# Order of work in a delta rule chunk's first slots, the first output projection's units begun on the attention's features, and a bias table's transfers in eight parts

## The chip, the cores and the metric

One NeuronCore of a Trainium2 chip runs the whole program. The metric is the device time of one execution in microseconds, lower is better. TensorE is written PE here, its weight loads PEld, VectorE is DVE, ScalarE is ACT, GpSimd is POOL and SyncE is SP.

## The reference, cut to what matters

Three transformer blocks are run one after the other on 1024 tokens of 1024 features, all in float32. The first block matters here:

```
x = layer_norm(x);  h = x @ w_in
o_gdn = gated_delta_rule(q, k, v, g, beta), forward and backward in time, 4 heads of 128, then rms_norm * silu(z)
o_na  = neighborhood_attention(q, k, v, rpb), 16 rows of 64 tokens, 8 heads of 64, then rms_norm
x = layer_norm(alpha * x + concat(o_gdn, o_na) @ w_out);  x = layer_norm(alpha * x + relu(x @ w1 + b1)^2 @ w2 + b2)
```

In a chunk of the delta rule a unit lower triangular system is solved, then `o = q_dec S + qk v_new` and `S = S * g_last + k_dec^T v_new`. The second block has a sliding window attention whose score bias is a table looked up by distance (`rel_bias[bucket]`). It is laid out once, long before it is used.

## The kernel before

Every large matrix product is cut into *units*: 128x1024 weights, fetched by SP into one of four slots (`load_sp`, L252), split into a high part on ACT (`split_act`, L257) and a low part on DVE (`split_dve`, L262), and multiplied in three passes (high by high, high by low, low by high): 24 matmuls of 512 columns (L299) for an output unit. A slot's next load is issued when PE has done the unit in it, so loads run four units ahead. Splits run two units ahead (`AHEAD`). `walk` writes each engine's instruction stream from one list of steps. Every engine works its own stream strictly in order, and the streams meet at semaphores.

**The mixers.** Between the first input projection and the first output projection PE works two mixers interleaved in slots. The delta rule (`gdn_pe`, `gdn_act`, `gdn_dve`) has 8 steps `n` of 14 slots `s`; each step handles one 128-token chunk for both directions: `d = 0` takes chunk `n`, `d = 1` takes chunk `7 - n`. The attention (`na_pe`, `na_act`, `na_dve`) takes one of the 16 rows every 7 slots. Each direction has three PSUM banks, `gbank(d, 0)` to `gbank(d, 2)`. In a chunk's slots:

- slot 12 and 13: prepare the next chunk's decay and `A`, solve for `v_new` (`V`, copied to `g_vn` by ACT, L1121);
- slot 0: PE forms the output of the *previous* chunk (`o`, L1020 and L1021, 16 matmuls a direction, bank 1) and its state update (`su`, 4 matmuls, bank 0), then turns the new `A` (bank 2, L1007). DVE copies or adds the output (L1138, L1141), updates the state `g_S` (L1146), and then forms the first level of the inverse from the turned `A` (`lev`, L1152, and `Dt`, L1158);
- odd slots 1 to 11, levels `l` = 1 to 6: PE turns `Dt` (bank 0, L1007) and multiplies by `A` (`Q`, bank 1, L1001), ACT copies the turned part (`g_D`, L1097), DVE masks `Q` (L1164). Even slots 2 to 12: PE forms `X` (bank 2, L1001), DVE subtracts it from `Dt` (L1171).

On PE the turn of level 1 waits for `Dt`, so behind it stands all of PE's later work. From the second half of the chunks on, a third thread (`gout`) normalises finished chunks beside this (sums L1428 on PE, L1432 and L1434 on ACT). Slot 0 of `n` = 6 and 7 has such a piece.

**The end of the mixers.** In the last slot (`n = 8`, slot 0) the last outputs and the last attention row are formed. Then `end1_pe`, `end1_act` and `end1_dve` normalise the last three chunks (`out_sq`, `out_sum`, `out_rs`, `out_norm`; chunk 0, then 6, then 7) and split the mixed features of the first 512 tokens, then of the last 512, into high and low parts (`mix1_hi` on ACT, L1475; `mix1_lo` on DVE, L1481). Features 4 to 7 of 8 are the attention's and come first in `MIX_ORDER`; 0 to 3 are the delta rule's. Only behind all this do ACT and DVE split the first weights of `out1[0]`, the output projection's eight units of the first half, which PE then works. SP issues, ahead of those weights and on the same queue, the 4 MB of residual (`xT<-x`, L1584).

**The bias table.** `t5_pool` runs on POOL. It broadcasts an 8-partition table into an internal DRAM tensor by one DMA (1.5 MB, L1635), waits, and reads it back skewed by one DMA (1 MB, L1638). DVE waits for it 38 units after PE made the table (L1657).

Of the kernel before, what the change touches and what calls it, by code (L numbers as in the profile page):

```python
# [14 lines left out]
P = 128  # L15
# [105 lines left out]
def build_program(nc, g):  # L121

    ctx = ExitStack()
    with ctx:
# [78 lines left out]
        class Unit:  # L203

            def __init__(self, kind, src=None, half=0, j=0, gr=0, pool="bg", meta=False, gate=None):
                self.kind, self.src, self.half, self.j, self.gr, self.pool = kind, src, half, j, gr, pool
                self.meta, self.gate, self.n = meta, gate, None
                self.ks, self.back, self.whole = range(DC), None, kind in WHOLE
# [60 lines left out]
        def unit_pe(pe, u):  # L269
            if u.kind == "nv1":  # L270
                nv1_pe(pe, u)
                return
            if u.use:
                pe.wait_ge(bank_free(u), u.use)
# [4 lines left out]
            if u.kind == "down":  # L279
# [10 lines left out]
                return  # L290
            for h in range(2) if u.whole else [u.half]:
                spans = [(0, W // 2), (W // 2, W)] if u.meta else [(META, W)]
                for i_k, k in enumerate(u.ks):
# [7 lines left out]
            last.then_inc(mm_done[u.z], 1)  # L301
# [646 lines left out]

        def level(n, d, l):

            return 2 * NL * n + 2 * l + d + 1
# [41 lines left out]
        def gdn_pe(pe):  # L993
# [15 lines left out]

            pe.wait_ge(nv_act, 4)  # L1010
            pe.wait_ge(nv_dve, 4)
            for n, s in gdn_slots():
                m, l = n - 1, (s + 1) // 2
                if s == 0 and n:
                    for d in (0, 1) if n < TC else (1, 0):
                        pe.wait_ge(gs["vn"], once(m, d))
                        pe.wait_ge(gs["qd"], once(m, d))
                        for h in range(GH):
                            o = pbank(gbank(d, 1))[:, h, :]
                            nc.tensor.matmul(o, g_S[d][:, h, :], g_qd[d][:, h, :], start=True, stop=False)  # L1020
                            last = nc.tensor.matmul(o, g_vn[d][:, h, :], g_qk[d][:, m % 2, h, :], start=False, stop=True)  # L1021
                        last.then_inc(gs["o"], 1)
                        if n < TC:
                            pe.wait_ge(gs["eg"], once(n, d))
                            pe.wait_ge(gs["t0"], once(n, d))
                            pe.wait_ge(gs["kd"], once(m, d))
                            heads(gbank(d, 0), g_kd[d], g_vn[d]).then_inc(gs["su"], 1)
                if s == 0 and n < TC:
                    for d in range(2):
                        pe.wait_ge(gs["A"], once(n, d))  # L1030
                        turned(gbank(d, 2), g_A[d]).then_inc(gs["AT"], 1)
                if 1 <= s <= 12 and s % 2 and n >= 0:
                    for d in range(2):
                        pe.wait_ge(gs["Dt"], level(n, d, l - 1))
                        if l == 1:
                            pe.wait_ge(gs["S"], once(n, d))
# [4 lines left out]
                        turned(gbank(d, 0), g_Dt[d]).then_inc(gs["tr"], 1)  # L1041
# [2008 lines left out]
```

## Time and profile before

| | |
|---|---|
| three timed runs | 4097.46, 4099.32, 4105.66 us (median 4099.32) |
| the profiled execution | 4106.44 us, of which 4104.7 us span |
| PE busy | 3958.7 us, 96% of the span |
| DVE, ACT busy | 2167.2 us, 1676.0 us |
| mean granted clock of PE | 0.985 |
| delta rule's and attention's slots | about 421 to 966 us of the span |
| end of the mixers to the output projection's first matmul | about 966 to 992 us |

A busy share says how long an engine had an instruction in work, not that it went at full speed: PEclk, the granted clock, has two levels, and at 0.50 a matmul takes twice as long though PE counts as fully busy. In a timeline a line gives the start, the time taken, engine, source line, operation and count; in brackets stand the engine's idle time before it and what ended that.

### The profile page before, as it was taken

What the parts mean: (1) busy time and instruction counts of PE and PEld (TensorE: products, weight loads), DVE (VectorE), ACT (ScalarE), POOL (GpSimd) and SP (SyncE); (2) the same over time, 40 slices, a digit from 0 to 9 for tenths busy, and PEclk for the clock granted to TensorE, in tenths of its full rate; (3) what the DMA queues carried; (4) which work ended last, traced back from release to release, by engine and by line L of the source; (5) the groups of instructions that cost most, each with busy time, mean ns of one, the idle gap of its engine ahead of it and who ended that gap; (6) DMA issues with size and microseconds to landing.
All of it is one profiled execution on the core that took longest, in us unless ns stands there. A gap on an engine that the chain in (4) does not pass through costs nothing.

```text
span 4104.7 us, 47331 instructions
## 1 busy us (share of the span) xinstructions
PE 3958.7 (96%) x19500; PEld 3228.7 (79%) x19500; DVE 2167.2 (53%) x3208; ACT 1676.0 (41%) x2626; POOL 9.9 (0%) x20
## 2 busy tenths in 40 slices
PE   4999999997989999999999999999999999999999
PEld 2777888986778877887787878987778777778887
DVE  6541444554643355784657855436656445645334
ACT  3351555565433354433534444333334233334333
POOL 0000000000000000000000000000000000000000
PEclk9999998998999999999999999999999999999999
DMA  4112000002243222222222222222222222223322
GB/s 165 52 62 63 10 5 5 13 24 100 82 103 97 93 88 93 77 84 86 87 93 78 78 93 92 89 89 81 77 84 96 89 91 78 78 87 114 97 93 87
DMA packets 113565, 323.44 MB, mean 79 GB/s; under 512 B 26656, under 2 KB 33712, under 8 KB 113352
## 3 DMA queue, kind: packets, MB, share of 16 engines
q1 hardware_dynamic: 111416, 314.91, 23.9%
q0 software_dynamic: 1936, 5.51, 0.7%
q8 instruction: 156, 2.56, 0.3%
q14 instruction: 57, 0.47, 0.0%
HBM read 303.86 MB, written 18.06 MB: 78 GB/s over the span
## 4 chain that ended last, share of the span: by engine, by line
PE 90%; DVE 5%; ACT 3%; issue 1%; DMA 1%; SPq 0%; DVEq 0%; ACTq 0%
PE ps L299 48%; PE ps L286 25%; PE ps L1001 4%; PE ps L1269 1%; PE ps L1007 1%; PE ps L712 1%; PE ps L1246 1%; PE ps L2354 1%; PE ps L996 1%; PE ps L1254 1%; PE ps L1794 1%; PE ps L408 1%; DMA w_raw<-in_w_mlp 1%; DVE a L495 0%; DVE xT L348 0%
## 5 line engine op out<-in xcount | busy, mean ns | idle before, releaser
L299 PE MATMUL ps<-a,w_hi 128*128 128x512 f32 (+1 forms) x6128 | 1879.3, 391 | 33.2 <-issue 15.1
L299 PEld LDWEIGHTS ps<-a,w_hi 128*128 128x128 f32 x6128 | 1128.5, 189 | 309.4 <-issue 37.3
L299 PE MATMUL ps<-a,w_lo 128*128 128x512 f32 (+1 forms) x3064 | 1164.7, 387 | 0.0
L262 DVE TENSOR_TENSOR w_lo<-w_raw,w_hi 128x1024 fp32r<-128x1024 f32 x539 | 658.1, 1221 | 461.3 <-ACT w_hi L257 458.5
L257 ACT ACTIVATE w_hi<-w_raw 128x1024 fp32r<-128x1024 f32 x539 | 563.7, 1050 | 593.2 <-DMA w_raw<-in_w_mlp 367.0
L299 PEld LDWEIGHTS ps<-a,w_lo 128*128 128x128 f32 x3064 | 572.2, 189 | 123.0
L286 PE MATMUL ps<-h_hi,w_hi 128*128 128x512 f32 x1536 | 490.5, 401 | 1.9 <-DVE xT L348 1.9
L286 PE MATMUL ps<-h_hi,w_lo 128*128 128x512 f32 x1536 | 481.4, 395 | 0.0
L286 PE MATMUL ps<-h_lo,w_hi 128*128 128x512 f32 x1536 | 481.2, 395 | 0.0
L343 DVE TENSOR_TENSOR h_lo<-u_sq,h_hi 128x512 fp32r<-128x512 f32 x192 | 132.9, 692 | 486.5 <-ACT h_hi L333 486.5
L348 DVE TENSOR_TENSOR xT<-xT,ps 128x1024 f32<-128x1024 f32 x192 | 234.2, 1220 | 287.4 <-PE ps L286 286.5
L286 PEld LDWEIGHTS ps<-h_hi,w_hi 128*128 128x128 f32 x1536 | 285.9, 189 | 73.2 <-issue 5.8
L286 PEld LDWEIGHTS ps<-h_hi,w_lo 128*128 128x128 f32 x1536 | 289.7, 189 | 66.0
L286 PEld LDWEIGHTS ps<-h_lo,w_hi 128*128 128x128 f32 x1536 | 289.8, 189 | 65.6
L328 ACT ACTIVATE u_act<-ps 128x512 f32<-128x512 f32 x128 | 76.4, 597 | 366.2 <-PE ps L299 366.1
L1767 DVE SCALAR_TENSOR_TENSOR mixh<-c_pad,params,mixh 128x512 f32<-128x512 f32 x240 | 163.7, 744 | 0.0
L332 ACT ACTIVATE u_sq<-u_act 128x512 f32<-128x512 f32 x192 | 121.4, 632 | 17.8 <-ACT u_act L328 0.4
L328 ACT ACTIVATE u_act<-ps,params 128x512 f32<-128x512 f32 x64 | 44.0, 688 | 202.9 <-PE ps L299 202.9
L333 ACT ACTIVATE h_hi<-u_act 128x512 fp32r<-128x512 f32 x192 | 118.0, 615 | 0.0
L354 DVE TENSOR_TENSOR xT<-xT,ps 128x512 f32<-128x512 f32 x48 | 33.0, 687 | 147.0 <-PE ps L299 147.0
L1001 PEld LDWEIGHTS ps<-g_gu,g_D 128*128 128x128 f32 x768 | 96.9, 202 | 9.5 <-issue 9.3
L1001 PE MATMUL ps<-g_Dt,g_A 128*128 128x64 f32 x768 | 98.5, 285 | 0.0
(358 smaller groups left out, 3359.8 us busy)
## 6 DMA issues: line engine op xcount, KB each, us to landing
w_raw<-in_w_mlp SPq DMA_DIRECT2D x384, 512.0 KB, 3.4
w_raw<-in_w_in SPq DMA_DIRECT2D x107, 512.0 KB, 3.5
w_raw<-in_w_out SPq DMA_DIRECT2D x48, 512.0 KB, 3.4
xT<-in_x SPq DMA_DIRECT2D x2, 2048.0 KB, 12.3
x<-xT SPq DMA_DIRECT2D x2, 2048.0 KB, 7.6
xT<-x SPq DMA_DIRECT2D x2, 2048.0 KB, 12.9
rpb_rows<-in_rpb SPq DMA_DIRECT2D x1, 3810.0 KB
z<-staged SPq DMA_DIRECT2D x4, 512.0 KB, 3.8
```

Of the source, the lines that this page charges most:

```text
L257: nc.scalar.activation(w_hi[u.z][:, :], w_raw[u.z][:, :], ACT.Copy).then_inc(w_hi_done[u.z], 1)
L262: nc.vector.tensor_tensor(w_lo[u.z][:, :], w_raw[u.z][:, :], w_hi[u.z][:, :].bitcast(F32), ALU.subtract).then_inc(w_split[u.z], 1)
L286: last = nc.tensor.matmul(ps[:, u.bank + c, :], w[:, k * 256 + c * P:k * 256 + (c + 1) * P], act[:, (u.first + k) % RING, :], start=(k == ...
L299: last = nc.tensor.matmul(ps[:, bank, 0:t1 - t0], w[:, k * P:(k + 1) * P], a[:, h, low, k, t0:t1], start=(i_k == 0 and i == 0), stop=(i_k ...
L328: nc.scalar.activation(u_act[:, s, :], ps[:, u.bank, :], ACT.Relu, bias=bias).then_inc(bank_free(u), 1)
L332: nc.scalar.activation(u_sq[:, s, :], u_act[:, s, :], ACT.Square)
L333: nc.scalar.activation(h_hi[:, u.chunk % RING, :], u_act[:, s, :], ACT.Square).then_inc(hid_hi, 1)
L343: nc.vector.tensor_tensor(h_lo[:, r, :], u_sq[:, u.chunk % 2, :], h_hi[:, r, :].bitcast(F32), ALU.subtract)\
L348: nc.vector.tensor_tensor(two, two, ps[:, u.bank:u.bank + 2, :], ALU.add).then_inc(bank_free(u), 1)
L408: nc.tensor.matmul(ps[:, bank, :], const("ones"), m.q[:, 0, :], start=True, stop=True).then_inc(m.s["sum"], 1)
L1001: last = nc.tensor.matmul(halves(pbank(b), l, which)[:, h], lhsT[:, h, :], halves(rhs[:, :, :], l, which)[:, h], start=True, stop=True)
L1767: nc.vector.scalar_tensor_tensor(y, x, w, y, op0=ALU.mult, op1=ALU.add).then_inc(c_tap, 1)
```

## The change

Five edits. (1) Slot 0: PE works output of `d = 0`, the two turns of `A`, output of `d = 1`, then both state updates; DVE forms `lev` and `Dt` before outputs and state. Since the banks then collide, level 1 uses bank 2 for its turn and bank 1 for `X`, and the wait for the state moves from level 1 to level 2. (2) In the last chunk direction 1 comes first in slot 13, so that chunk 0 is ready first. (3) The order of the attention's rows changes so that the first half's are done after 12 rows; in slot 13 of the last chunk ACT and DVE split the attention's features of the first half and the weights of the first two units of `out1[0]`; after the first sum of `end1`, PE works the first half (four of eight feature blocks) of three units, then the two other sums; later those units are completed. The third unit moves to the bank pool "fg". (4) Each unit of `out1` waits for its feature blocks one by one. (5) The bias table is written by eight DMAs, each waiting for the one before, and read by eight.

```diff
+            if u.taken:
+                unit_part(pe, u, u.taken, DC)
                 return
...
+        def unit_part(pe, u, first, stop):
+
+            if first == 0 and u.taken:
+                if u.use:
+                    pe.wait_ge(bank_free(u), u.use)
+                pe.wait_ge(w_split[u.z], u.turn + 1)
             for h in range(2) if u.whole else [u.half]:
                 spans = [(0, W // 2), (W // 2, W)] if u.meta else [(META, W)]
-                for i_k, k in enumerate(u.ks):
+                for i_k in range(first, stop):
+                    k = u.ks[i_k]
...
+        def both_ways(n):
+
+            return (1, 0) if n == TC - 1 else (0, 1)
+
+        def last_once(n, d):
+            return once(n, 1 - d if n == TC - 1 else d)
+
+        def turn_bank(d, l):
+            return gbank(d, 2 if l == 1 else 0)
+
+        def cross_bank(d, l):
+            return gbank(d, 1 if l == 1 else 2)
...
+            def step_out(m, d):
+                pe.wait_ge(gs["vn"], last_once(m, d))
+                pe.wait_ge(gs["qd"], once(m, d))
+                for h in range(GH):
+                    o = pbank(gbank(d, 1))[:, h, :]
+                    nc.tensor.matmul(o, g_S[d][:, h, :], g_qd[d][:, h, :], start=True, stop=False)
+                    last = nc.tensor.matmul(o, g_vn[d][:, h, :], g_qk[d][:, m % 2, h, :], start=False, stop=True)
+                last.then_inc(gs["o"], 1)
+
+            def step_turned(n, d):
+                pe.wait_ge(gs["A"], once(n, d))
+                turned(gbank(d, 2), g_A[d]).then_inc(gs["AT"], 1)
...
-                if s == 0 and n:
-                    for d in (0, 1) if n < TC else (1, 0):
-                        pe.wait_ge(gs["vn"], once(m, d))
-                        pe.wait_ge(gs["qd"], once(m, d))
-                        for h in range(GH):
-                            o = pbank(gbank(d, 1))[:, h, :]
-                            nc.tensor.matmul(o, g_S[d][:, h, :], g_qd[d][:, h, :], start=True, stop=False)
-                            last = nc.tensor.matmul(o, g_vn[d][:, h, :], g_qk[d][:, m % 2, h, :], start=False, stop=True)
-                        last.then_inc(gs["o"], 1)
-                        if n < TC:
-                            pe.wait_ge(gs["eg"], once(n, d))
-                            pe.wait_ge(gs["t0"], once(n, d))
-                            pe.wait_ge(gs["kd"], once(m, d))
-                            heads(gbank(d, 0), g_kd[d], g_vn[d]).then_inc(gs["su"], 1)
-                if s == 0 and n < TC:
+                if s == 0 and n == 0:
                     for d in range(2):
-                        pe.wait_ge(gs["A"], once(n, d))
-                        turned(gbank(d, 2), g_A[d]).then_inc(gs["AT"], 1)
...
+                if s == 0 and 0 < n < TC:
+                    step_out(m, 0)
+                    step_turned(n, 0)
+                    step_turned(n, 1)
+                    step_out(m, 1)
+                    for d in range(2):
+                        pe.wait_ge(gs["eg"], once(n, d))
+                        pe.wait_ge(gs["t0"], once(n, d))
+                        pe.wait_ge(gs["kd"], once(m, d))
+                        heads(gbank(d, 0), g_kd[d], g_vn[d]).then_inc(gs["su"], 1)
+                if s == 0 and n == TC:
+                    step_out(m, 1)
+                    step_out(m, 0)
                 if 1 <= s <= 12 and s % 2 and n >= 0:
                     for d in range(2):
                         pe.wait_ge(gs["Dt"], level(n, d, l - 1))
-                        if l == 1:
+                        if l == 2:
                             pe.wait_ge(gs["S"], once(n, d))
                         if l == 4:
                             pe.wait_ge(gs["R"], once(n, d))
                         if l == 6:
                             pe.wait_ge(gs["kd"], once(n, d))
-                        turned(gbank(d, 0), g_Dt[d]).then_inc(gs["tr"], 1)
+                        turned(turn_bank(d, l), g_Dt[d]).then_inc(gs["tr"], 1)
...
-                        half_heads(gbank(d, 2), g_D[d], g_gu[d], l, 1 - d).then_inc(gs["X"], 1)
+                        half_heads(cross_bank(d, l), g_D[d], g_gu[d], l, 1 - d).then_inc(gs["X"], 1)
...
+                if s == 13 and n == TC - 1:
+                    act.wait_ge(n_copied, 16 * len(HELD))
+                    act.wait_ge(na["of"], NP * 3)
+                    mix1_hi(act, 0, (0, 1, 2, 3))
+                    split_act(act, ahead1[0])
+                    split_act(act, ahead1[1])
...
-                if s == 0 and n:
-                        dve.wait_ge(gs["o"], 2 * TC - d if n == TC else once(m, d))
...
-                            ins.then_inc(gs["S"], 1)
...
+                if s == 0 and n:
+                    for d in both_ways(m):
+                        dve.wait_ge(gs["o"], last_once(m, d))
+                        out = g_o[:, :, toks(chunk_of(m, d))]
+                        if m < TC // 2:
+                            nc.vector.tensor_copy(out, pbank(gbank(d, 1))).then_inc(gs["oe"], 1)
+                        else:
+                            dve.wait_ge(gs["oe"], TC)
+                            nc.vector.tensor_tensor(out, out, pbank(gbank(d, 1)), ALU.add).then_inc(gs["oe"], 1)
+                if s == 0 and 0 < n < TC:
+                    for d in range(2):
+                        dve.wait_ge(gs["su"], once(m, d))
+                        dve.wait_ge(gs["S"], once(m, d))
+                        for h in range(GH):
+                            ins = nc.vector.scalar_tensor_tensor(g_S[d][:, h, :], g_S[d][:, h, :], gcol(G_LAST, m, d, h),
+                                                                 pbank(gbank(d, 0))[:, h, :], op0=ALU.mult, op1=ALU.add)
+                        ins.then_inc(gs["S"], 1)
...
+                if s == 13 and n == TC - 1:
+                    mix1_lo(dve, 0, (0, 1, 2, 3))
+                    split_dve(dve, ahead1[0])
...
-        CHUNKS = [0, 7, 1, 6, 5, 3, 4, 2]
+        CHUNKS = [0, 7, 1, 6, 2, 3, 4, 5]
-        HELD = {c: i for i, c in enumerate([5, 6, 1, 0, 7])}
+        HELD = {c: i for i, c in enumerate([2, 6, 1, 0, 7])}
...
         def end1_pe(pe):
-            for i in (5, 6, 7):
+            out_sum(pe, 5, SUM_BANKS[5])
+            for u in ahead1:
+                unit_part(pe, u, 0, DC // 2)
+            for i in (6, 7):
                 out_sum(pe, i, SUM_BANKS[i])
 
         def end1_act(act):
             out_sq(act, 5, 2 * TC - 1)
-            act.wait_ge(gs["o"], 2 * TC)
-            act.wait_ge(n_copied, 16 * len(HELD))
-            act.wait_ge(na["of"], ROWS)
-            mix1_hi(act, 0, (0, 1))
+            split_act(act, ahead1[2])
+            out_sq(act, 6, 2 * TC - 1)
             out_rs(act, 5, SUM_BANKS[5])
-            mix1_hi(act, 0, (2, 3))
-            out_sq(act, 6, 2 * TC - 1)
             out_sq(act, 7, 2 * TC)
             act.wait_ge(go["end"], 6)
             mix1_hi(act, 0, (4, 5, 6, 7))
             out_rs(act, 6, SUM_BANKS[6])
             out_rs(act, 7, SUM_BANKS[7])
+            act.wait_ge(gs["o"], 2 * TC)
+            act.wait_ge(na["of"], ROWS)
             mix1_hi(act, 1, (0, 1, 2, 3))
             act.wait_ge(go["end"], 8)
             mix1_hi(act, 1, (4, 5, 6, 7))
 
         def end1_dve(dve):
-            mix1_lo(dve, 0, (0, 1))
+            split_dve(dve, ahead1[1])
+            split_dve(dve, ahead1[2])
             out_norm(dve, 5)
-            mix1_lo(dve, 0, range(2, DC))
+            mix1_lo(dve, 0, (4, 5, 6, 7))
             out_norm(dve, 6)
             out_norm(dve, 7)
             mix1_lo(dve, 1, range(DC))
...
-            nc.gpsimd.dma_start(g["t5_rows"], s_rows[:, :].unsqueeze(1).to_broadcast([HQ, P, 384])).then_inc(t5_row, 16)
-            pool.wait_ge(t5_row, 16)
-            src = bass.AP(g["t5_rows"].tensor, g["t5_rows"].offset + P - 1, [[384 - 1, P], [P * 384, HQ], [1, 2 * WIN]])
-            nc.gpsimd.dma_start(s_bias[:, :, :], src).then_inc(t5_row, 16)
+
+            for i in range(HQ):
+                part = slice(P // HQ * i, P // HQ * (i + 1))
+                if i:
+                    pool.wait_ge(t5_row, 16 * i)
+                nc.gpsimd.dma_start(g["t5_rows"][:, part], s_rows[:, :].unsqueeze(1).to_broadcast([HQ, P // HQ, 384])).then_inc(t5_row, 16)
+            for i in range(HQ):
+                pool.wait_ge(t5_row, 16 * (HQ + i))
+                src = bass.AP(g["t5_rows"].tensor, g["t5_rows"].offset + i * P * 384 + P - 1, [[384 - 1, P], [1, 2 * WIN]])
+                nc.gpsimd.dma_start(s_bias[:, i, :], src).then_inc(t5_row, 16)
...
-            dve.wait_ge(t5_row, 32)
+            dve.wait_ge(t5_row, 32 * HQ)
...
+                u.gate = mix_gate(0)
+        out1[0][2].pool = "fg"
+        for u in out1[0][:3]:
+            u.taken = DC // 2
+            ahead1.append(u)
...
-                    split(eng, u)
+                    if u not in ahead1:
+                        split(eng, u)
...
-                if split is not None and u.n is not None and u.n + AHEAD < stop:
+                if split is not None and u.n is not None and u.n + AHEAD < stop and order[u.n + AHEAD] not in ahead1:
```

## Rows read from the trace of the kernel before

**Rows 1.** the page's chain that ended last, shares of the span by engine

```profile
PE 90%; DVE 5%; ACT 3%; issue 1%; DMA 1%; SPq 0%; DVEq 0%; ACTq 0%
```

**Rows 2.** waits of PE over the span: us in total, times, longest

```profile
PE ps L1007 <- DVE g_Dt L1158: 14.5, 8, 2.0
```

**Rows 3.** busy time and granted clock (PEclk) by stretch, around chunk starts

```profile
496.00:508.00 12.00, 12.00 (x67) 12.00 (x66) 2.19 (x6) 5.37 (x11) 0.00 (x0) 0.57 0.01 2
...
564.00:573.00 9.00, 9.00 (x53) 9.00 (x54) 1.80 (x5) 3.79 (x8) 0.00 (x0) 0.62 0.00 0
...
701.00:715.00 14.00, 13.90 (x68) 13.91 (x69) 2.16 (x7) 5.79 (x13) 0.00 (x0) 0.51 0.00 1
...
840.00:852.00 12.00, 9.72 (x83) 8.90 (x81) 6.07 (x17) 10.75 (x21) 0.00 (x0) 1.00 0.01 2
```

**Rows 4.** timeline of slot 0 and 1, n = 4: start, us, engine, line

```profile
696.62 0.17 DVE L1373 TENSOR_SCALAR n_small<-n_small 128x4 f32<-128x4 f32 x1
...
698.11 1.00 PE L1294 MATMUL ps<-consts,n_z 128*128 128x64 f32 x8
...
699.96 0.75 DVE L1152 TENSOR_TENSOR g_gu<-ps,g_lev 128x256 f32<-128x256 f32 x2
...
701.10 1.97 PE L1007 MATMUL ps<-consts,g_Dt 128*128 128x128 f32 x8 [1.99 <-DVE g_Dt L1158]
```

**Rows 5.** timeline of slot 1 and 2, n = 6

```profile
842.18 1.09 PE L1007 MATMUL ps<-consts,g_Dt 128*128 128x128 f32 x8 [1.73 <-DVE g_Dt L1158]
...
845.30 1.07 ACT L1097 ACTIVATE g_D<-ps 128x512 f32<-128x512 f32 x2
...
846.02 1.97 PE L1001 MATMUL ps<-g_gu,g_D 128*128 128x64 f32 x16
```

**Rows 6.** timeline of the end of the mixers

```profile
956.89 10.41 SPq L252 DMA_DIRECT2D w_raw<-in_w_out  x4
...
961.08 1.28 ACT L1334 ACT_TABLE_LOAD   x1
...
965.33 1.10 PE L1294 MATMUL ps<-consts,n_z 128*128 128x64 f32 x8 [0.38 <-DVE n_z L1395]
...
968.52 1.28 ACT L1432 ACT_TABLE_LOAD   x1
...
973.26 0.69 DVE L1442 TENSOR_TENSOR mixT<-mixT,g_qT 128x512 f32<-128x512 f32 x1
...
974.05 3.67 PE L1428 MATMUL ps<-g_vt,consts 128*128 128x512 f32 x4 [5.41 <-ACT g_vt L1424]
...
992.05 1.19 PE L299 MATMUL ps<-a,w_hi 128*128 128x512 f32 x2 [14.32 <-issue]
```

**Rows 7.** DMA issues of 936 to 1000: count, KB each, us to landing

```profile
w_raw<-in_w_out SPq DMA_DIRECT2D x4, 512.0 KB, 12.9
```

**Rows 8.** chain of work, 1040 to 1115: start, us, what

```profile
1045.92 16.71 PE ps L299 x72
```

**Rows 9.** the page's groups: count, busy us, mean ns, idle before

```profile
L262 DVE TENSOR_TENSOR w_lo<-w_raw,w_hi 128x1024 fp32r<-128x1024 f32 x539 | 658.1, 1221 | 461.3 <-ACT w_hi L257 458.5
...
L257 ACT ACTIVATE w_hi<-w_raw 128x1024 fp32r<-128x1024 f32 x539 | 563.7, 1050 | 593.2 <-DMA w_raw<-in_w_mlp 367.0
```

**Rows 10.** the page's DMA issues of POOL, median us to landing

```profile
t_rows<-s_rows POOLq DMA_DIRECT2D x1, 1536.0 KB, 35.6
...
s_rel<-in_rel_bias POOLq DMA_DIRECT2D x1, 1.0 KB, 1.8
```

**Rows 11.** DMA issues of 1184 to 1190: count, KB each, us to landing

```profile
w_raw<-in_w_mlp SPq DMA_DIRECT2D x1, 512.0 KB, 22.2
```

**Rows 12.** timeline, 1198 to 1218

```profile
1212.12 1.22 PE L299 MATMUL ps<-a,w_hi 128*128 128x512 f32 x2 [9.23 <-DVE xT L348]
```

**Rows 13.** granted clock after that wait

```profile
1212.00:1216.00 4.00, 3.88 (x9) 3.11 (x10) 0.06 (x1) 0.26 (x1) 0.00 (x0) 0.50 0.49 84
```

**Rows 14.** bias table: ns min/median/max, first and last start

```profile
L1657 DVE TENSOR_TENSOR s_bias<-s_bias,s_mask x1: 2284/2284/2284, 1406.6 to 1406.6; 128x2048 f32<-128x2048 f32 x1
```

More of the change, by code:

```diff
@@ L207, in __init__ @@
                 self.meta, self.gate, self.n = meta, gate, None
-                self.ks, self.back, self.whole = range(DC), None, kind in WHOLE
+                self.ks, self.back, self.whole, self.taken = range(DC), None, kind in WHOLE, 0
         WHOLE = ("ab1", "cv1", "z1", "nq1", "nk1")
@@ L272, in unit_pe @@
                 return
+            if u.taken:
+                unit_part(pe, u, u.taken, DC)
+                return
             if u.use:
@@ L300, in unit_pe @@
                                                     start=(i_k == 0 and i == 0), stop=(i_k == DC - 1 and i == 2))
-            last.then_inc(mm_done[u.z], 1)
+            if stop == DC:
+                last.then_inc(mm_done[u.z], 1)
         def unit_out(u):
@@ L1068, in gdn_pe @@
                 if s == 13 and n >= 0:
-                    for d in range(2):
+                    for d in both_ways(n):
                         pe.wait_ge(gs["R"], once(n, d))
@@ L1096, in gdn_act @@
                         act.wait_ge(gs["tr"], upper(n, d, l))
-                        nc.scalar.activation(four(g_D[d][:, :, :]), ps[:, gbank(d, 0), :], ACT.Copy).then_inc(gs["D"], 1)
+                        nc.scalar.activation(four(g_D[d][:, :, :]), ps[:, turn_bank(d, l), :], ACT.Copy).then_inc(gs["D"], 1)
                 if s == 4 and n >= 0:
@@ L1117, in gdn_act @@
                 if s == 13:
-                    for d in range(2):
+                    for d in both_ways(n):
                         if n >= 0:
-                            act.wait_ge(gs["V"], once(n, d))
+                            act.wait_ge(gs["V"], last_once(n, d))
                             nc.scalar.activation(four(g_vn[d][:, :, :]), ps[:, gbank(d, 1), :], ACT.Copy).then_inc(gs["vn"], 1)
@@ L1170, in gdn_dve @@
                         part = halves(g_Dt[d][:, :, :], l, 1 - d)
-                        nc.vector.tensor_tensor(part, part, halves(pbank(gbank(d, 2)), l, 1 - d), ALU.subtract).then_inc(gs["Dt"], 1)
+                        nc.vector.tensor_tensor(part, part, halves(pbank(cross_bank(d, l)), l, 1 - d), ALU.subtract).then_inc(gs["Dt"], 1)
                 if s == 3 and n >= 0:
@@ L1482, in mix1_lo @@
                                         ALU.subtract).then_inc(mix_ready[h], 1)
+        ahead1 = []
         def end1_pe(pe):
[L1485 removed]
+            out_sum(pe, 5, SUM_BANKS[5])
+            for u in ahead1:
+                unit_part(pe, u, 0, DC // 2)
+            for i in (6, 7):
                 out_sum(pe, i, SUM_BANKS[i])
```

15 lines of the change are left out of this document (2 added, 13 removed).

## The prediction

> **What bounds the kernel now.** I read the page first: the chain that ended last runs through PE for 90% of the span [rows 1], and PE is busy for 96%. So time is saved only where PE stands still or runs at its lower clock, and each such place is worth its own length. The waits of PE and the table of stretches then show which places the change touches.
>
> First, the start of a chunk. PE waits for `Dt` at level 1 eight times, 14.5 us in total, 2.0 at most [rows 2]: the 1.99 us of [rows 4] recur for `n` = 1 to 5, `n` = 6 and 7 have 1.73 each [rows 5], and the rest is `n` = 0. The wait has a second price. Right behind each of the five 2.0 us waits the granted clock falls from 2.4 to 1.2 GHz: 0.57 over 12 us (`n` = 1 and again 3), 0.62 over 9 us (`n` = 2 and again 5), 0.51 over 14 us (`n` = 4), with PE busy throughout [rows 3]. Behind the two waits of 1.73 us it does not fall (1.00 over 12 us). The work lost is width times (1 - clock): 5.2 + 3.4 + 5.2 + 6.9 + 3.4 = 24.1 us.
>
> Second, the end of the mixers: PE stands 14.32 us before the output projection and a few microseconds twice before that, and starts it at 992.05 [rows 6].
>
> Third, the bias table. Its write takes 35.6 us [rows 10]; a weight load issued meanwhile takes 22.2 us to land [rows 11], and PE waits 9.23 us for a unit of the first MLP [rows 12]. The row puts that on DVE's `xT` at L348, but DVE was itself behind the late split. After it PE runs 4 us at 0.50 [rows 13].
>
> **Starts of chunks, edit 1.** Before, DVE was free of the attention at 696.8 (696.62 + 0.17), spent until 699.96 on outputs and state (3.2 us for two copies and two updates), and released PE 1.14 us later, at 701.10; PE had done its last other work at 699.1 (698.11 + 1.00) [rows 4]. After, `lev` and `Dt` come first: released at 696.8 + 1.14 = 697.9, which is 1.2 us before PE is done. PE's own work in the slot is the same instructions in another order. So the 1.99 us go. What is late next: DVE now does the 3.2 us behind both `Dt`, until about 701.7, and masks `Q` of level 1 only then; `X` needs that. At full clock turn to `X` takes 3.84 us (842.18 to 846.02, [rows 5]), so PE wants `X` at about 702.6 and DVE delivers at about 702.5. That is close, so I charge 0.3 us a chunk. `n` = 1 to 5: 5 x (2.0 - 0.3) = 8.5 us. The unknown is between 0 (all of the wait reappears) and 10.
>
> At `n` = 6 and 7 I expect nothing. There ACT is behind with the normalisation and copies the turned part at 845.30 [rows 5]; `X` at 846.02 hangs on that copy, before and after. The 1.73 us move from before the turn to before `X`.
>
> The clock: with no 2 us standstill left, I take the whole 24.1 us back. Ends: 0 if it falls anyway; and a loss at `n` = 6 and 7, if their new standstill is enough, of 3.4 to 6.9 us each [rows 3].
>
> **The end of the mixers, edits 2 to 4.** The first half of three units is 3 x 4 x 3 = 36 matmuls of 16.71 / 72 = 0.232 us [rows 8], 8.4 us of work that had no place before. What stands in front of it: ACT, in slot 13, now waits for the first weights of `out1[0]`. They are issued at 956.89 [rows 6] and land 12.9 us later [rows 7], behind the residual on the same queue, at 969.8; that cannot come sooner, since SP's order is the same. Behind the waiting instruction on ACT stand the square root chain of the last attention row, and through it DVE's outputs, the last row's sum and all of `end1`. Two splits of 1.05 us [rows 9] take ACT to about 972.0. Before, the same chain started at 961.08 and reached PE's L1294 at 965.33, 4.2 us [rows 6]; now PE has that at 976.2, 10.9 us later. From there: L1294 at the lower clock to 978.0, the squares to 979.1, the first sum, half of 3.67 us [rows 6], to 981.0. Then the 36 matmuls. The clock stands low there; before, it needed 4 to 6 us of work to rise, so some 6 matmuls take twice as long (2.8 us) and the others 7.0: done at 990.8. Then come the two other sums, 0.9 each at full clock: 991.7 and 992.6. The chain from a sum through both table loads to the end of the norm took 973.95 - 968.52 = 5.4 us [rows 6], so chunk 0 is split well before that and PE goes on with the second halves of the three units until 992.6 + 8.4 = 1001.0.
>
> Now the price of putting the sums behind the matmuls. ACT and DVE can norm chunks 6 and 7 only from 991.7 on (Ln, load, Exp 2.6 us, then 3.9 for the next: 998.2; norm 1.5), DVE then splits eight blocks of the second half at 0.61 each (half of L262's width, [rows 9]), 999.7 to 1004.6, finishes one eviction of 0.69, and splits the fourth unit's weights in 1.22: 1006.5. PE stands from 1001.0 to 1006.5 and then has five units of 24 x 0.232 = 5.57, and about 2.1 us of loss from a low clock again: 1036.5. Before: 992.05 + 8 x 5.57 + 2.8 for the low clock = 1039.4. Gain 2.9 us. Ends: if PE does not have to stand at 1001, 1028.9, a gain of 10.5; if the clock stays low for all 36 matmuls (8.4 more, handed on by the sums), less 5.5. The gates per block in edit 4 are waits that the first unit already had; I charge nothing. The third unit's other bank pool shifts which banks later units use; nothing bounds that from a row but the smallness of PE's waits there, and I allow 2 us either way.
>
> **The bias table, edit 5.** The unit before the late one ended where the 9.23 us began, so a load may take 22.2 - 9.2 = 13.0 us to land without harm. A piece has a fixed part near 1.8 us (the 1 KB table, [rows 10]) and an eighth of the rest, 4.2 us. A load that meets a piece waits at most out that 4.2 and then goes alone while the next is being issued: 4.2 + 3.4, the median landing, is 7.6, under 13.0. So the wait goes, and with it the low clock, 4 x 0.5 = 2.0 [rows 13]: 11.2 us. Ends: 0 and 11.2. The chain of eight writes and eight reads takes, with some 1 us to issue each, over 80 us in all, and is hidden: DVE asks for the table only at 1406.6 [rows 14], nearly 200 us after the wait at 1212.
>
> The Trainium skill, DMA: Bandwidth & Descriptors, "Anatomy of one DMA", puts a fixed part of about 2.0 us on each DMA issued from GpSimd and advises to batch; that speaks against cutting one into eight. The 1.8 us of [rows 10] agree. By its figure the sixteen would cost 14 x 2 = 28 us more, an estimate, all of it on POOL's own chain, so the sum stays.
>
> **Sum.** 8.5 + 24.1 + 2.9 + 11.2 = 46.7 us, from the profiled execution's 4106.4 (4104.7 of span and 1.7 around it): 4059.7. That execution is 7.1 us over the median of the timed runs. The lengths of the low clock vary, and with all five at the shortest seen (17.0 instead of 24.1) it would have taken 4099.3, the median. Then the change gives 39.6, and the result is again 4059.7. I forecast 4060.
>
> **Rivals.**
>
> *The clock falls all the same.* PE's small waits around level 1 remain and the low stretches stay. For it: at full clock PE also waits a little later in the slot. Against it: five of five falls follow the 2.0 us wait, none the 1.73. Time: 4060 + 17 to 24, about 4081.
>
> *It falls in new places.* The moved standstill at `n` = 6 and 7 becomes two falls of 3.4 to 6.9: 4067 to 4074, about 4070.
>
> *The weights stay late.* While a piece runs it may hold a load back as the whole did, and pieces follow closely. For it: 22.2 us is much more than a fair share. Against it: the gap after every piece. 11.2 us stay: 4071. The Trainium skill (the same page, "Queues, rings and completion order") says that each DMA engine takes turns between queues packet by packet; by that, size changes nothing as long as a piece is in work. No row shows the gaps.
>
> *The slower one.* In `t5_pool` the time of a write could depend on its 8 source partitions and not on its bytes. Then each piece takes as long as the whole, and each brings its own late unit: 8 x 11.2 = 90 us instead of 11.2 before, 4060 + 90 = 4150. It would decide from the fourth such wait on, since the rest gives 35.5 us. For it: 1.5 MB in 35.6 us is slow, since a 0.5 MB load lands in 3.4. Against it: the 1 KB table took 1.8 us.
>
> **Chances and range.** Forecast 0.58; clock falls all the same 0.12; new places 0.14; weights late 0.09; slower 0.03; the end of the mixers better by its upper bound (4052) 0.04. The range 4046 to 4083 holds all but the slower one, the ends of the unknowns together included (-8 at the end stage, -2 banks). Anything within 0.2% (8 us, about what a measurement can tell from no change) would need several rivals at once: 0.03. Faster 0.93, slower 0.04.
>
> **What would show it.** Right: no wait L1007 on L1158 at `n` = 1 to 7; PEclk 1.00 from 485 to 840; ACT standing some 6 us for `w_out` weights in the last chunk; PE standing near the fourth output unit with "w_lo" late; no 9 us wait in the first MLP, loads landing under 13 us. Wrong: PEclk still near 0.6 behind a chunk's start, PE idle before `X` at every `n`, or a landing of 22 us again.

## The result and the profile after

The changed kernel took 4059.85 us (median of 4 runs, 4052.51 to 4063.38) where the kernel before took 4098.39 beside it (4 runs, 4090.92 to 4105.66): a ratio of 0.9904, 95% interval 0.9881 to 0.9926. On another chip it was 4059.32 against 4094.88, 0.9905 (0.9889 to 0.9922). It is faster by some 37 us, 0.95%; 4060 was forecast.

The page of the changed kernel, its chain by engine and by line (before: [rows 1]):

```profile
PE 92%; DVE 4%; ACT 2%; DMA 1%; issue 1%; SPq 0%; DVEq 0%; ACTq 0%
PE ps L311 49%; PE ps L289 25%; PE ps L1027 4%; PE ps L1022 2%; PE ps L1316 1%; PE ps L1033 1%; PE ps L1293 1%; PE ps L725 1%; PE ps L2412 1%; PE ps L1301 1%; PE ps L1852 1%; PE ps L421 1%; DVE a L508 0%; PE ps L1103 0%; PE ps L1341 0%
```

PE still bounds the kernel, with 92% instead of 90%. The waits of PE from 400 to 1100 us (us in total, times, longest):

```profile
PE ps L1341 <- DVE n_z L1442: 11.4, 1, 11.4
...
PE ps L311 <- issue: 5.6, 1, 5.6
PE ps L1027 <- ACT g_D L1134: 2.9, 2, 1.4
...
PE ps L1033 <- DVE g_Dt L1185: 1.1, 1, 1.1
```

The last row answers to [rows 2]: of eight waits for `Dt` at level 1 only `n` = 0's is left. The row of L1027 is new: before `X` PE waits 1.4 us for ACT at `n` = 6 and again at 7. The rows of L1341 and L311 are the end of the mixers, below.

The stretches behind each chunk's start, after (columns: window, its width, busy us of PE, PEld, DVE, ACT and POOL, PEclk, DMA share, GB/s); those of [rows 3] stood at 0.51 to 0.62:

```profile
480.00:495.00 15.00, 15.00 (x131) 14.39 (x130) 9.88 (x29) 13.91 (x33) 0.00 (x0) 1.00 0.04 10
544.00:558.00 14.00, 14.00 (x122) 13.40 (x122) 9.33 (x28) 12.88 (x30) 0.00 (x0) 1.00 0.05 11
...
734.00:748.00 14.00, 14.00 (x131) 14.00 (x129) 8.52 (x26) 12.10 (x29) 0.00 (x0) 1.00 0.05 11
799.00:813.00 14.00, 11.72 (x97) 10.67 (x96) 9.60 (x27) 13.26 (x30) 0.00 (x0) 1.00 0.01 1
864.00:890.00 26.00, 23.84 (x189) 22.43 (x188) 13.27 (x37) 20.49 (x44) 0.00 (x0) 0.93 0.00 1
```

In this execution the clock is full at `n` = 1 to 6, and 26 x 0.07 = 1.8 us are lost at `n` = 7; most others lose more there (see "Why the prediction was right"). The timeline of `n` = 6 shows what became of the 1.73 us of [rows 5] (start, duration, instruction, idle before it and its releaser):

```profile
802.38 0.75 DVE L1185 TENSOR_TENSOR g_Dt<-g_Dt,g_gu 128x256 f32<-128x256 f32 x2
...
804.21 1.04 PE L1033 MATMUL ps<-consts,g_Dt 128*128 128x128 f32 x8
...
807.43 1.09 PE L1301 MATMUL ps<-consts,n_s 128*128 128x128 f32 x8 [0.45 <-ACT g_vt L1479]
```

```profile
808.69 0.63 ACT L1481 ACTIVATE g_vt<-g_vt 128x512 f32<-128x512 f32 x1
809.23 1.07 ACT L1134 ACTIVATE g_D<-ps 128x512 f32<-128x512 f32 x2
...
809.95 1.97 PE L1027 MATMUL ps<-g_gu,g_D 128*128 128x64 f32 x16 [1.43 <-ACT g_D L1134]
```

DVE has `Dt` ready a microsecond before PE turns it at 804.21, so there is no wait. But ACT, behind with the gates, copies the turned part only at 809.23, and PE stands 0.45 + 1.43 us before `X`: the same standstill in a later place.

The end of the mixers, after (answers to [rows 6, 7]):

```profile
922.09 40.99 SPq L252 DMA_DIRECT2D w_raw<-in_w_out  x6
...
926.95 2.18 ACT L1522 ACTIVATE a<-mixT 128x512 fp32r<-128x512 f32 x4
...
934.93 1.06 ACT L257 ACTIVATE w_hi<-w_raw 128x1024 fp32r<-128x1024 f32 x1 [5.80 <-DMA w_raw<-in_w_out]
...
941.49 1.97 PE L1341 MATMUL ps<-consts,n_z 128*128 128x64 f32 x8 [11.44 <-DVE n_z L1442]
...
945.62 1.84 PE L311 MATMUL ps<-a,w_hi 128*128 128x512 f32 x2
...
955.26 1.88 PE L1475 MATMUL ps<-g_vt,consts 128*128 128x512 f32 x4
```

```profile
969.74 1.21 DVE L262 TENSOR_TENSOR w_lo<-w_raw,w_hi 128x1024 fp32r<-128x1024 f32 x1
...
971.05 1.19 PE L311 MATMUL ps<-a,w_hi 128*128 128x512 f32 x2 [5.55 <-issue]
```

ACT stands 5.80 us for the first `w_out` weights, and everything queued behind it comes late: PE waits 11.44 us for the last attention row. The first halves of three units fill the time to 955.26, where the second and third sums follow at full clock. PE then finishes the three units and stands 5.55 us, until DVE has split the fourth unit's weights at 969.74 + 1.21.

The bias table: the DMA issues from 1130 to 1215 us (KB each, median us to landing; answers to [rows 10, 11]):

```profile
w_raw<-in_w_mlp SPq DMA_DIRECT2D x15, 512.0 KB, 3.7
t_rows<-s_rows POOLq DMA_DIRECT2D x8, 192.0 KB, 5.7
s_bias<-t_rows POOLq DMA_DIRECT2D x8, 128.0 KB, 2.8
```

The slowest weight load in it took 6.3 us, and the 9.23 us of [rows 12] are gone. Before, not one load but all four that were issued during the write took 16 to 24 us; the first of them, the 22.2 of [rows 11], made PE wait. The new landing times follow the pieces: loads issued 4.9, 3.5, 2.5 and 1.4 us after a piece was issued landed after 3.4, 4.2, 5.2 and 6.3 us. So a load that meets a piece waits out much of what is left of it, and no more.

Where each profiled execution spent its time (us): "slots" from the first to the last output matmul of the delta rule; "end" from there to the first sum of the norm; "to table" until the bias table's matmul; "table" from there until DVE adds the mask to it. The kernels `e1_slots` to `e9_both` are those of the experiments below. An execution that was profiled need not be the median one: that of after is the fastest of its four, that of `e9_both` the slowest of its four.

| kernel | slots | end | to table | table | span |
|---|---|---|---|---|---|
| before | 479.1 | 80.4 | 134.9 | 226.8 | 4104.7 |
| e1_slots | 447.5 | 79.4 | 132.6 | 227.4 | 4072.3 |
| e2_slots_table | 449.1 | 79.4 | 132.6 | 215.3 | 4057.6 |
| e3_table | 467.5 | 80.3 | 134.9 | 215.3 | 4081.9 |
| e4_filler | 456.2 | 79.5 | 134.8 | 226.5 | 4078.7 |
| e5_dve_order | 474.1 | 78.3 | 134.9 | 215.3 | 4081.8 |
| e6_no_gaps | 449.1 | 79.2 | 134.0 | 233.9 | 4078.8 |
| after | 446.4 | 76.6 | 132.7 | 215.3 | 4050.7 |
| after, again | 448.9 | 79.2 | 134.0 | 215.4 | 4061.3 |
| e7_late_split | 446.2 | 69.7 | 134.0 | 215.4 | 4051.1 |
| e8_fourth | 449.2 | 72.1 | 135.7 | 215.4 | 4055.5 |
| e9_both | 448.7 | 62.9 | 135.7 | 215.4 | 4049.5 |

### The profile page after: what moved, and what is told of

Read it like the earlier page. It is cut to its first block, busy times and chain, and to the rows that moved or that the text cites. A ratio compares the mean times of both kernels' runs of the same rounds, so it can differ in the third digit from the quotient of the medians.

```text
span 4050.7 us, 47347 instructions
## 1 busy us (share of the span) xinstructions
PE 3928.2 (97%) x19500; PEld 3204.4 (79%) x19500; DVE 2166.8 (53%) x3208; ACT 1673.7 (41%) x2626; POOL 17.1 (0%) x34
## 4 chain that ended last, share of the span: by engine, by line
PE 92%; DVE 4%; ACT 2%; DMA 1%; issue 1%; SPq 0%; DVEq 0%; ACTq 0%
PE ps L311 49%; PE ps L289 25%; PE ps L1027 4%; PE ps L1022 2%; PE ps L1316 1%; PE ps L1033 1%; PE ps L1293 1%; PE ps L725 1%; PE ps L2412 1%; PE ps L1301 1%; PE ps L1852 1%; PE ps L421 1%; DVE a L508 0%; PE ps L1103 0%; PE ps L1341 0%
## 5 line engine op out<-in xcount | busy, mean ns | idle before, releaser
L311 PE MATMUL ps<-a,w_hi 128*128 128x512 f32 (+1 forms) x6128 | 1875.2, 391 | 14.9 <-DVE a L508 6.7
L311 PEld LDWEIGHTS ps<-a,w_hi 128*128 128x128 f32 x6128 | 1126.3, 189 | 287.3 <-issue 27.5
L311 PE MATMUL ps<-a,w_lo 128*128 128x512 f32 (+1 forms) x3064 | 1163.4, 386 | 0.0
L311 PEld LDWEIGHTS ps<-a,w_lo 128*128 128x128 f32 x3064 | 571.3, 189 | 122.9
L1027 PEld LDWEIGHTS ps<-g_gu,g_D 128*128 128x128 f32 x768 | 91.0, 192 | 12.1 <-issue 11.9
L1027 PE MATMUL ps<-g_gu,g_D 128*128 128x64 f32 x768 | 92.2, 273 | 2.9 <-ACT g_D L1134 2.9
```

The lines of the kernel that those rows point to most:

```text
L311: last = nc.tensor.matmul(ps[:, bank, 0:t1 - t0], w[:, k * P:(k + 1) * P], a[:, h, low, k, t0:t1], start=(i_k == 0 and i == 0), stop=(i_k ...
L1027: last = nc.tensor.matmul(halves(pbank(b), l, which)[:, h], lhsT[:, h, :], halves(rhs[:, :, :], l, which)[:, h], start=True, stop=True)
```

## The experiments

**One part alone.** `e1_slots` is the kernel before with edit 1, `e3_table` with edit 5, `e2_slots_table` with both.

```diff
  e1_slots: step_out / step_turned / DVE's lev and Dt first / banks of level 1; nothing else
  e3_table: eight writes, each behind the one before, and eight reads; nothing else
  e2_slots_table: both; end1_pe, end1_act, end1_dve, CHUNKS and slot 13 as before
```

> The kernel before with edit 1 alone (order and banks of slot 0). My theory: the 2.0 us waits for Dt at level 1 go, and because PE no longer stands still there the granted clock stays at 1.00 behind them; 24 us of low clock and 8.5 us of waits in the profiled run, so 25 to 33 us less than before (the low stretches vary from run to run). The wait of the first MLP (9.2 us) and the 14 us stand at the end of the mixers stay. Rival (the clock falls for another reason, for instance because of the small matmuls of slots 1 and 2): PEclk stays near 0.6 behind the chunk starts and the gain is 8 to 10 us.

> The kernel before with edit 5 alone (bias table written and read by eight DMAs). My theory: weight loads land in under 13 us while the pieces run, the 9.2 us wait and the 4 us of low clock behind it go: 11 us less. Rival (a load waits as long behind a piece): landings near 22 us and no gain. Rival (the eight pieces hold more loads back): slower.

> Edits 1 and 5 on the kernel before, that is the changed kernel without edits 2 to 4 (end of the mixers). If the parts add up: the sum of the gains of the two kernels with one edit, 36 to 44 us, and 3 to 5 us slower than the changed kernel. Rival (edits 2 to 4 are worth nothing or lose, since PE then stands 5.6 us at the fourth unit): equal to the changed kernel or faster.

These three and `e4_filler` ran on one chip beside the kernel before (4095.61, 15 runs). `e1_slots` 4073.85, ratio 0.9948 (0.993 to 0.9966), 21.8 us less, with the waits of 14.2 and 9.3 us at the end of the mixers and in the first MLP still there; `e3_table` 4082.34, 0.9966 (0.9954 to 0.9978), 13.3 less, its slowest weight load beside the pieces 6.8 us and the 9.2 us wait gone; `e2_slots_table` 4061.67, 0.9918 (0.99 to 0.9937), 33.9 less, and 21.8 + 13.3 is 35.1. So the two edits add up, though to less than the 36 to 44 expected. Edit 1 came out under the 25 expected: that rested on a profiled execution with much low clock, and edit 1 brings some low clock of its own (both below). Edits 2 to 4 are what is left; they were not run alone. 4061.67 against 4059.85 and 4059.32 is some 2 us, and the gains over the kernel before on each chip, 33.9 against 38.5 and 35.6, differ by 1.7 to 4.6. These runs can't tell that from nothing.

**The standstill and the clock apart.** `e4_filler` is the kernel before, with three matmuls of 384 columns at the start of each chunk whose results nobody reads. They run just where PE would stand, so DVE is as late as before, but PE does not stand.

```diff
+                    if p == 4 and i > 14 and i % 14 == 4:
+                        pe.wait_ge(na["m"], NP * k + NP)
+                        for _ in range(3):
+                            nc.tensor.matmul(ps[:, 6, 0:384], const("ident"), consts[:, 0:384], start=True, stop=True)
```

> The kernel before, unchanged in its order, with three matmuls of 384 columns on PE (about 1.9 us, their result is not used) at the end of slot 0 of chunks 1 to 7, just where PE waits for Dt. If the standing still is what brings the clock down: PE waits under 0.3 us there, the turn of level 1 starts at the same moment as before, PEclk stays at 1.00 behind it, and the kernel is 17 to 24 us faster than before though it does more work and waits for Dt as long. Rival (the clock falls for another reason): PEclk near 0.6 as before, and the time is the same or up to 2 us longer.

4080.31 (4079.83 to 4081.76), ratio 0.9963 (0.9951 to 0.9975): 15.3 us less than before, by added work; 17 to 24 had been expected, again from the profiled execution. Its six runs lie within 1.9 us of each other, the fifteen of the kernel before beside them within 20 (4087.58 to 4107.64): with the standstill most of the spread is gone there. Three of the five stretches of [rows 3], now:

```profile
496.00:508.00 12.00, 12.00 (x104) 11.52 (x103) 4.64 (x12) 5.60 (x15) 0.00 (x0) 1.00 0.01 2
564.00:573.00 9.00, 9.00 (x73) 8.17 (x72) 3.59 (x8) 3.71 (x11) 0.00 (x0) 1.00 0.01 2
...
701.00:715.00 14.00, 13.92 (x113) 12.59 (x111) 8.69 (x34) 6.59 (x12) 0.00 (x0) 1.00 0.05 11
```

The clock is at its upper level (2.4 GHz) everywhere there: where these standstills are filled it does not fall. The filler itself, in PE's row at `n` = 5 (three matmuls, two records each), lasts 2.15 us:

```profile
748.82 2.15 PE L1280 MATMUL ps<-consts 128*128 128x384 f32 x6
```

So `e4_filler` pays 2.15 us a chunk in the place of the 2.0, and no low clock; it cuts edit 1's gain in two. The first output matmul of each chunk, `n` = 1 to 7, and the length of chunks 1 to 6 from it:

```
before        485.4 554.8 622.5 691.9 763.1 832.3 899.9   69.4 67.7 69.4 71.2 69.2 67.6
e3_table      484.2 550.3 614.7 679.2 750.3 819.5 887.1   66.1 64.4 64.5 71.1 69.2 67.6
e5_dve_order  482.8 550.5 618.3 687.6 755.7 824.9 892.4   67.7 67.8 69.3 68.1 69.2 67.5
e4_filler     483.6 548.1 612.5 677.0 741.7 807.6 875.2   64.5 64.4 64.5 64.7 65.9 67.6
e1_slots      485.8 548.1 610.4 672.6 735.2 798.9 867.7   62.3 62.3 62.2 62.6 63.7 68.8
after         483.2 545.4 607.7 670.0 732.5 796.2 863.8   62.2 62.3 62.3 62.5 63.7 67.6
after, again  484.1 546.4 608.6 670.9 733.5 797.1 867.3   62.3 62.2 62.3 62.6 63.6 70.2
```

From before to `e4_filler` chunks 1 to 5 shrink by 4.9, 3.3, 4.9, 6.5 and 3.3, in all 22.9 us, and with 5 x 0.15 for the longer filler that is 23.7 us of low clock. From there to after they shrink by 11.0, about 5 x 2.15, and so by 2.0 us of standstill in each. Chunk 6 gives nothing here and costs 2.6 us in the second execution, and chunk 7 gives 1.2 back (456.2 - 446.4 is 9.8, not 11.0).

The row of `e3_table` was a surprise: it has every wait of [rows 2], yet chunks 2 and 3 are as short as with the filler. Its stretches right around the waits of `n` = 3 and `n` = 4:

```profile
619.00:633.00 14.00, 12.01 (x110) 11.88 (x109) 7.49 (x24) 9.54 (x24) 0.00 (x0) 1.00 0.00 1
683.00:697.00 14.00, 12.02 (x73) 11.88 (x72) 6.49 (x20) 8.15 (x22) 0.00 (x0) 0.68 0.00 0
```

Both hold 2.0 us of standstill (14.00 less 12.01 and 12.02); the clock fell after the one and not after the other. So the clock falls in these places only where there is a standstill, and not always then.

**Which half of edit 1.** `e5_dve_order` is the changed kernel, PE's new order and banks kept, with DVE's outputs and state ahead of `lev` and `Dt` again.

```diff
 def gdn_dve, slot 0
-                if s == 0 and n < TC: (lev, Dt)
                 if s == 0 and n: (outputs, state)
+                if s == 0 and n < TC: (lev, Dt)
```

> The changed kernel with DVE's order of slot 0 as before (outputs and state, then lev and Dt); PE's order and the banks stay changed. My theory (DVE's order is what removes the wait): DVE needs both state updates first, which PE now forms last, so Dt comes later than before, the turn of level 1 waits 2.5 to 4 us at chunks 1 to 7, and PEclk falls to about 0.6 behind it: 40 us slower than the changed kernel or more. Rival (PE's order is what counts): waits under 1 us and no fall of the clock.

One run, 4083.62, 24 us above the changed kernel. Its wait and two of its stretches:

```profile
PE ps L1033 <- DVE g_Dt L1202: 14.5, 8, 2.0
```

```profile
632.00:644.00 12.00, 12.00 (x75) 11.52 (x74) 3.04 (x8) 5.05 (x12) 0.00 (x0) 0.71 0.01 1
701.00:715.00 14.00, 14.00 (x111) 13.63 (x111) 5.02 (x14) 5.70 (x14) 0.00 (x0) 0.90 0.00 1
```

The wait is that of [rows 2] to the digit, and the low clock costs 18.8 us (chunks 1 to 5 against `e4_filler`: 342.1 - 324.0, and 0.75 for the filler). Longer waits and a larger loss (40 us or more) had been expected; that was wrong. What follows stands: without DVE's order the gain is gone, and PE's order alone gives nothing. Whether DVE's order would do it without PE's is not shown.

**The gaps between the pieces.** `e6_no_gaps` is the changed kernel with the eight writes issued back to back.

```diff
-                if i:
-                    pool.wait_ge(t5_row, 16 * i)
```

> The changed kernel with the eight writes of the bias table issued back to back, without waiting for the one before; the reads still wait for all writes. If the gaps between the pieces are what lets the weight loads through (my prediction's reason): the writes are in work without a break for about 35 us, loads land in 15 to 22 us again and PE waits several us in the first MLP. Rival (the size of a piece or which DMA engines it falls on is what counts): loads land in under 10 us and PE does not wait.

One run, 4080.58. The issues of 1150 to 1170 us, and PE's longest wait in the first MLP:

```profile
q0 software_dynamic: 515, 1.06, 92.6%
q1 hardware_dynamic: 72, 0.26, 3.2%
...
w_raw<-in_w_mlp SPq DMA_DIRECT2D x4, 512.0 KB, 23.0
t_rows<-s_rows POOLq DMA_DIRECT2D x6, 192.0 KB, 22.1
```

```profile
PE ps L311 <- DVE xT L361: 16.3, 1, 16.3
```

The "table" stage is 233.9, 18.6 above the changed kernel and 7.1 above before. Cutting the write into pieces is worth nothing by itself; waiting for each piece to end is what lets the weights through. While pieces are always in work, the queue of POOL (q0) holds the 16 DMA engines for 92.6% of the time and the weight loads (q1) for 3.2%. For comparison, the kernel before, from 1190 to 1200 us, in the middle of its one write:

```profile
q0 software_dynamic: 106, 0.49, 49.2%
q1 hardware_dynamic: 133, 0.50, 16.0%
```

The one write holds half the engines' time, and the pieces back to back nearly all of it. So `e6_no_gaps` takes away the gaps and also puts more than one piece in work at once; which of the two makes it worse than before is not separated. That gaps are needed follows from before as well, where the engines were held for only half the time, but without a break, and four loads were late. The Trainium skill, DMA: Bandwidth & Descriptors, "Queues, rings and completion order", has the engines take turns packet by packet. In the kernel before the packets are near even (106 and 133), in `e6_no_gaps` they are not: 515 to 72, and from 1150 to 1160 us 261 to none, though a load had been issued at 1153.3. What holds the loads back there stays open. Even turns would not be even time either: by these rows a packet of the table's write is in work for 0.58 to 0.74 us and one of the weights for 0.14 to 0.19.

**The end of the mixers.** Two costs that the prediction named, taken away one by one. `e7_late_split` moves the splits of the first two units' weights behind the last attention row; `e8_fourth` splits the fourth unit's weights ahead of the norms of chunks 6 and 7; `e9_both` does both.

```diff
 e7_late_split: gdn_act / gdn_dve, slot 13, last chunk
-                    split_act(act, ahead1[0])
-                    split_act(act, ahead1[1])
-                    split_dve(dve, ahead1[0])
 end1_act, behind out_sq(act, 5, ...); end1_dve, first
+            split_act(act, ahead1[0])
+            split_act(act, ahead1[1])
+            split_dve(dve, ahead1[0])
 e8_fourth: end1_act / end1_dve, behind mix1_hi / mix1_lo(0, (4, 5, 6, 7))
+            split_act(act, ahead1[3])
+            split_dve(dve, ahead1[3])
+        fourth = out1[0][3]
+        fourth.pool = "fg"
+                pe.wait_ge(go["ln"], 8)   (its first matmul waits for the norms that read that bank)
```

> The changed kernel with the splits of the first two units' weights moved on ACT and DVE from slot 13 of the last chunk to behind the square of chunk 0 in the end stage. If ACT's wait for these weights (5.8 us, and two splits) is what delays the last attention row and all behind it: the 11.4 us wait of PE at the fold of the last row falls to about 3 us, the first sum and the 36 matmuls start about 8 us earlier, and so does the fourth unit: 6 to 9 us less. Rival (the end is bound by something later): 0 to 2 us.

> The changed kernel with the fourth unit's weights split by ACT and DVE before the norms of chunks 6 and 7 and not behind them, and that unit in a bank of its own. If the 5.6 us stand of PE before the fourth unit comes from its weights' split standing behind the second half's features: the stand goes (some 1 us may come at the fifth unit) and with it the low clock behind it: 5 to 7 us less. Rival (the features or the bank set it): the stand stays, no gain.

> The changed kernel with both moves in the end of the mixers: the first two units' splits behind the square of chunk 0, and the fourth unit's split ahead of the norms of chunks 6 and 7. If the two standstills are separate: PE waits about 3 us at the fold of the last row and not at the fourth unit, and the gains add up, 12 to 15 us less than the changed kernel. Rival (one hides the other, since the norms of chunks 6 and 7 and the second half's features then set the end): 6 to 8 us, as each alone.

> The changed kernel itself once more, on the same chip as the kernel with both moves: about 38 us less than before, and the mark against which the next one is read.

`e7_late_split` 4053.13 (ratio to before 0.9888, 0.9873 to 0.9903), `e8_fourth` 4053.19 (0.9886, 0.9868 to 0.9904), each 6 us under the changed kernel, which ran on other chips (the ratios, each to the kernel before on its own chip, differ by 0.0016 to 0.0019, 7 to 8 us). On one chip, `e9_both` 4042.72 (4040.17 to 4051.31; 0.9874, 0.9859 to 0.989) and the changed kernel 4059.32: 16.6 us less, where 12 to 15 were expected. It beats both kernels. PE's waits from 900 to 1030 us, first in `e7_late_split`:

```profile
PE ps L311 <- issue: 5.7, 2, 5.6
PE ps L1338 <- DVE n_z L1439: 3.3, 1, 3.3
```

in `e8_fourth`:

```profile
PE ps L1341 <- DVE n_z L1442: 12.3, 1, 12.3
...
PE ps L311 <- issue: 0.6, 1, 0.6
```

and in `e9_both`:

```profile
PE ps L1338 <- DVE n_z L1439: 3.3, 1, 3.3
...
PE ps L311 <- issue: 0.8, 2, 0.6
```

Each edit took the wait it was aimed at and left the other. The "end" stage fell from 76.6 and 79.2 to 69.7 and 72.1, and with both to 62.9. Against the 80.4 of the kernel before, the changed kernel thus wins 1.2 to 3.8 us of the 17.5 that its edits 2 to 4 are worth once both costs are gone.

## Why the prediction was right

*The waits at a chunk's start*, predicted 8.5 us: 10.0 at `n` = 1 to 5. The step that was off is the 0.3 us a chunk charged for a late `X`; it did not come. It rested on a slip: from the prediction's own numbers PE wants `X` at 699.1 + 3.84 = 702.9, not 702.6, and DVE's 702.5 is early enough. At `n` = 6 and 7 nothing was expected, and the waits only moved.

*The low clock*, 24.1: 23.7 in this profile. It is right for this execution and too large for most. `e3_table`, with the same waits, lost 467.5 - 456.2 + 0.8 = 12.1, in three of the five places, and `e5_dve_order` 18.8 in all five. In the timed runs edit 1 brought 21.8 us and the filler alone, which takes only the clock's part, 15.3. The prediction said that such lengths vary, and its lower sum (17.0) was nearer.

*"It falls in new places"*, the rival at 0.14, came true beside the forecast, at a smaller price. Eight profiled executions have edit 1 whole (after and after again, `e1_slots`, `e2_slots_table`, `e6_no_gaps`, `e7_late_split`, `e8_fourth`, `e9_both`). The clock fell at `n` = 6 in seven of them, all but that of after, and at `n` = 7 in seven, all but `e7_late_split`, for 1.7 or 3.4 us each time (windows of 10 us at 0.66 to 0.87); it was priced at 3.4 to 6.9. In the middle of the eight that is 5.1 us a run, where after shows 1.8. The kernel before, `e3_table` and `e5_dve_order`, with their one wait of 1.73 us there, show no fall in six cases, and neither does `e4_filler`, where no standstill is left. So what held for the wait of 1.73 us did not carry over to the moved standstill of 0.45 + 1.43 us. The second execution of the changed kernel, around `n` = 6 and 7:

```profile
810.00:820.00 10.00, 9.13 (x53) 9.16 (x54) 3.17 (x8) 5.97 (x13) 0.00 (x0) 0.66 0.01 2
...
880.00:890.00 10.00, 8.89 (x65) 8.76 (x66) 4.42 (x9) 6.64 (x15) 0.00 (x0) 0.83 0.01 2
```

*The end of the mixers*, 2.9: 3.8 in one profiled execution and 1.2 in the other; 2.8 and 0.2 against the kernels without edits 2 to 4. Step by step it went as told: weights landing 12.8 us after their issue (12.9), ACT standing 5.80 (some 6), PE's last attention row waited for 11.44 us where it was 0.38 before, 11.1 more (10.9), the 36 matmuls done in 9.6 us (9.8), the stand before the fourth unit 5.55 (5.5). That ACT's wait for the weights and the late split of the fourth unit each cost time, some 6 us alone and 16.6 together, is shown by `e7_late_split`, `e8_fourth` and `e9_both`.

*The bias table*, 11.2: 226.8 - 215.3 = 11.5 in the profiles, 13.3 (9 to 19 by its interval) in the timed runs. Pieces took 5.7 us where 1.8 + 4.2 = 6.0 was worked out; the slowest load 6.3 under the 7.6. The chain of sixteen transfers took 73.6 us (over 80 was said) where the two took 42.2, all of it on POOL and hidden. That pieces need the gaps was an argument in the prediction and is shown by `e6_no_gaps`, with the second piece in work as the open point above. The rival that weights stay late was right in what it says of pieces in work, and fell by the gaps. The slower case (each piece as long as the whole) fell: 5.7 against 35.6 us.

*The sum.* From profile to profile the time fell by 53.9 us, 4106.4 to 4052.5, and not by 46.7. The three places of the change make 48.0 of that: slots 32.7 (10.0 + 23.7 and the 1.2 given back), end 3.8, table 11.5. The other 6 lie in stretches that no edit is aimed at: 2.2 ahead of the first chunk's start (485.4 against 483.2, where `e1_slots` has 485.8), 2.2 in "to table", where the granted clock is 0.95 before and 0.97 after and one kernel, the changed one, shows 132.7 and 134.0 in its two executions, and 1.6 behind the table (2698.1 against 2696.5, where after again has 2699.7). The execution that was profiled after is 7.3 us under its median, that of before was 7.1 over. By medians the change gave 38.5 and 35.6 us, against the 39.6 that the prediction worked out for a usual execution. The mechanisms were right in the main, but that 4060 was met within a microsecond is partly luck: in the timed runs edit 1 brought 21.8 where 8.5 + 17.0 = 25.5 stood, the table 13.3 where 11.2 stood, and the medians of the kernel before alone lie from 4094.9 to 4099.7 from chip to chip.

## What to carry to other kernels

A 2 us standstill of TensorE in a busy loop cost its own length and, through the clock, 1.2 to 2.4 times as much again (12.1 to 23.7 us for five of them, by the execution); where it can't be removed, a few matmuls whose results nobody reads were cheaper than standing. Moving a standstill is not removing it: the one that went from before the turn to before `X` was about as long (1.9 us for 1.7) and yet began to cost clock. A wait that is put ahead of other work on an in-order engine is paid by all that is queued behind it: here moving two weight splits behind it gave back 6 us, and splitting one unit ahead of others' norms 6 more. A large background DMA beside loads that the bounding engine waits for can be cut into pieces, but each must wait for the one before: without that the pieces did more harm than the whole.

## What the runs showed of the hardware

- The clock's answer to one and the same standstill differs: after PE's 2.0 us at a chunk's start it fell in five of five cases of the kernel before, in three of five of `e3_table`, in five of five of `e5_dve_order`, and in none where 2.15 us of matmuls filled the gap. The work lost was 23.7, 12.1 and 18.8 us. What decides it stays open.
- At `n` = 6 and 7 one standstill of 1.73 us was followed by no fall in six of six cases, and standstills of 0.45 and 1.43 us with 1.1 us of work between them by a fall in fourteen of sixteen (0.66 to 0.87 over 10 us). Why the second is worse is not shown.
- Eight writes of 192 KB from eight source partitions, back to back, took 19.0 us each in the median and held the 16 DMA engines 92.6% busy for 66 GB/s of traffic in all; a 512 KB weight load issued among them landed after 23.0 us in the median and 29.3 at most, instead of 3.4. One write of 1.5 MB held them 49.2% busy (over 10 us in its middle) and took 35.6 us, about as long as the eight together (1148.4 to 1183.3).
